# Layer 0's heads 0 and 1 scored one weight chunk before the projection ends

## The reference, cut to what matters

```python
proj = rms_norm(h) @ w_in                      # layer 0: 1024 -> 3072 columns
aq, ak, av, rq, rk, rv, rg = split(proj)       # 8 MoBA heads of 64, 4 retention heads
a_out = softmax(mask(rotary(aq) @ rotary(ak).T / 8)) @ av      # 256 tokens are one block: causal attention
r_out = group_norm((rot(rq) @ rot(rk).T * decay) @ rv) * silu(rg)
h = h + concat(a_out, r_out) @ w_out
h = h + hierarchical_moe(rms_norm(h))          # top 1 of 4 groups, top 2 of its 8 experts
```

## Time and profile before

| | |
|---|---|
| time of the runs, median of 3 | 1108.76 us (1108.43 to 1109.37) |
| the profiled execution, its own time | 1110.2 us |
| its span, first to last instruction | 1108.4 us |
| TensorE's mean granted clock | 0.910 of full speed |
| busy: PE, DVE, ACT, POOL | 903.1, 416.5, 243.8, 41.9 us |
| moved by the DMA engines | 440.73 MB, mean 398 GB/s |

### The profile page before, as it was taken

How to read it: one execution, slowest core, us unless ns; L and a number is a source line. 1 busy time by engine, 2 the same in 40 slices (tenths; PEclk the granted TensorE clock), 3 DMA queues, 4 the chain that set the end, 5 groups by cost and what they waited for, 6 DMA issues and landing times.

```text
span 1108.4 us, 21929 instructions
## 1 busy us (share of the span) xinstructions
PE 903.1 (81%) x9146; PEld 593.1 (54%) x9146; DVE 416.5 (38%) x1006; ACT 243.8 (22%) x622; POOL 41.9 (4%) x65
## 2 busy tenths in 40 slices
PE   9999989978685867677799998999676858585875
PEld 6877745645353535353488676656443525353532
DVE  6888433332222222222288665333221222222222
ACT  5567311100000000000265863111010000000012
POOL 0012200000000000000000312000000000000000
PEclk9999989989887888788999999999887978888899
DMA  9898999999999999999998668999999999999995
GB/s 353 251 402 334 358 410 429 427 429 429 429 428 428 429 427 429 429 429 428 408 386 345 233 270 356 427 427 429 427 430 429 427 428 430 427 428 430 429 426 234
DMA packets 56577, 440.73 MB, mean 398 GB/s; under 512 B 12113, under 2 KB 12625, under 8 KB 31058
## 3 DMA queue, kind: packets, MB, share of 16 engines
q1 hardware_dynamic: 56240, 440.02, 95.7%
q10 hardware_dynamic: 290, 0.07, 0.0%
HBM read 439.03 MB, written 1.05 MB: 397 GB/s over the span
## 4 chain that ended last, share of the span: by engine, by line
PE 49%; DMA 35%; SPq 5%; another core or an unknown queue 3%; DVE 3%; ACT 2%; issue 1%; POOL 0%; POOLq 0%; ACTq 0%; DVEq 0%
DMA ring<-in_w_expert_up 27%; PE banks L1138 14%; DMA ring<-in_w_expert_down 7%; PE banks L1166 6%; PE banks L1106 6%; PE banks L1179 3%; PE banks L1015 3%; PE banks L1019 3%; PE banks L1016 3%; SPq L524 2%; SPq L472 1%; PE banks L1232 1%; PE banks L1234 1%; PE banks L1233 1%
## 5 line engine op out<-in xcount | busy, mean ns | idle before, releaser
L1138 PE MATMUL banks<-ring,scratch 128*32 128x256 f32 x4096 | 287.2, 443 | 129.2 <-DMA ring<-in_w_expert_up 128.8
L1138 PEld LDWEIGHTS banks<-ring,scratch 128*32 128x32 f32 x4096 | 150.3, 127 | 260.2 <-issue 122.2
L1665 DVE TENSOR_SCALAR scratch<-scratch 128x128 f32<-128x128 f32 x64 | 14.5, 227 | 510.3 <-ACT scratch L779 507.6
L1166 PE MATMUL banks<-ring,xn 128*32 128x256 f32 x2048 | 137.0, 410 | 7.7 <-DMA ring<-in_w_expert_down 7.5
L778 ACT ACTIVATE scratch<-banks 128x128 f32<-128x128 f32 x64 | 17.8, 278 | 511.1 <-PE banks L1138 499.7
L1106 PEld LDWEIGHTS banks<-scratch,h 128*128 128x128 f32 x448 | 107.7, 334 | 5.8 <-issue 5.8
L1106 PE MATMUL banks<-scratch,h 128*128 128x128 f32 x448 | 110.4, 405 | 0.0
L1179 PE MATMUL banks<-xn 32*128 32x256 f32 x1024 | 74.8, 403 | 36.5 <-ACT xn L788 36.5
L1166 PEld LDWEIGHTS banks<-ring,xn 128*32 128x32 f32 x2048 | 63.6, 116 | 60.0 <-issue 23.1
L1179 PEld LDWEIGHTS banks<-xn 32*128 32x128 f32 x1024 | 50.3, 186 | 67.8 <-issue 67.7
L1440 DVE SCALAR_TENSOR_TENSOR split<-ring,gains,split 128x512 fp32r<-128x512 f32 x96 | 69.7, 765 | 24.1 <-ACT split L826 23.3
(11 more groups left out here) (177 smaller groups left out, 792.9 us busy)
## 6 DMA issues: line engine op xcount, KB each, us to landing
ring<-in_w_expert_gate SPq DMA_DIRECT2D x62, 2048.0 KB, 45.5
ring<-in_w_expert_up SPq DMA_DIRECT2D x61, 2048.0 KB, 48.8
ring<-in_w_expert_down SPq DMA_DIRECT2D x56, 2048.0 KB, 47.5
ring<-in_w_in_even SPq DMA_DIRECT2D x5, 2048.0 KB, 17.8
ring<-in_w_expert_down SPq DMA_DIRECT2D x10, 1024.0 KB, 10.0
ring<-in_w_in_odd SPq DMA_DIRECT2D x5, 2048.0 KB, 19.7
ring<-in_w_expert_up SPq DMA_DIRECT2D x6, 1024.0 KB, 11.0
ring<-in_w_out_even SPq DMA_DIRECT2D x2, 2048.0 KB, 9.0
```

The costliest lines, as they stand in the source:

```text
L1138: last = pe.matmul(psum[6][32 * j:32 * j + 32, 0:2 * P].rearrange("p (a s) -> p a s", a=2), xT[:, c, SLOTS * k:SLOTS * k + SLOTS], ring[:, ...
L1166: last = pe.matmul(psum[4][32 * q:32 * q + 32, 0:QUARTER], hidT[k][:, 32 * j:32 * j + 32], ring[:, DOWN_AT[k], D * j + QUARTER * q:D * j + ...
```

## The change

Five edits, all in layer 0:

- PE: `scores(0, 0)` stands between chunks 6 and 7 of block 5 instead of behind chunk 7. The wait for the retention scores' banks moves from it to `scores(0, 2)`.
- The two pairs of PSUM banks are swapped for layer 0: heads 0, 1, 4 and 5 in banks 4 and 5, the others in banks 0 and 1. Layer 1's stay as they are.
- DVE: `head_max` 0 and 1 stand ahead of `swish(1, 1)`. Behind it come `head_sum` 0 and 1 and the other maxima and sums in a changed order.
- ACT: exponentials 0 and 1 stand ahead of the `block_out` of block 5, as in layer 1.
- DVE: the gate of the retention's first half (four instructions) stands in one piece behind `head_sum` 7; before, two of the four stood ahead of it.

```diff
--- before.py
+++ after.py
@@ -451,7 +451,7 @@
             return psum[4 + 2 * t + q if ph % 2 == 0 else 2 * (1 - t) + q]
 
         def score_bank(l, m):
-            return psum[m % 2 + (0 if m // 2 % 2 == 0 else 6 if l else 4)]
+            return psum[m % 2 + ((0 if m // 2 % 2 == 0 else 6) if l else (4 if m // 2 % 2 == 0 else 0))]
 
         def mix_bank(n, t):
             return psum[t if n == 0 else 6 + t]
@@ -857,7 +857,7 @@
                             split_hT(l, t, 1)
                     else:
                         parts(0, 4)
-                    if l and j == NW:
+                    if j == NW:
                         for m in range(2):
                             exponentials(l, m)
                     if j > ROTATED[l]:
@@ -885,8 +885,7 @@
                     parts(COPY_AT[1], C)
 
                 if l == 0:
-                    for m in range(3):
-                        exponentials(l, m)
+                    exponentials(l, 2)
                     for m in range(5):
                         exponentials(l, m + 3)
                         copy_pT(l, m)
@@ -1044,7 +1043,7 @@
 
                 if m >= 4:
                     pe.wait_ge(s_out[l], m - 2)
-                elif l == 0 and m == 0:
+                elif l == 0 and m == 2:
                     pe.wait_ge(ret_ready, RET)
                 heads = [(score_bank(l, n), slice(HEAD * (n % 2), HEAD * (n % 2) + HEAD)) for n in (m, m + 1)]
                 q, k = qT[:, m // 2, :], kT[:, m // 2, :]
@@ -1301,9 +1300,12 @@
                     if l == 0 and j == NW - 1:
                         for i in range(2, RET):
                             item_scores(l, i)
-                    project(l, j, TURN_AT[1], C)
+                        project(l, j, TURN_AT[1], C - 1)
+                        scores(l, 0)
+                        project(l, j, C - 1, C)
+                    else:
+                        project(l, j, TURN_AT[1], C)
                 if l == 0:
-                    scores(l, 0)
                     scores(l, 2)
                     for b in range(2, 4):
                         pe.wait_ge(bank_out[l][b], 3)
@@ -1746,30 +1748,29 @@
                     swish(1, 0, link)
                     for n in range(2, RET):
                         decayed(n)
+                    for m in range(2):
+                        head_max(l, m)
                     swish(1, 1, link)
                 else:
                     dve.wait_ge(const_loaded[3], 16)
                 if l == 0:
-                    for m in range(3):
+                    for m in range(2):
+                        head_sum(l, m, link)
+                    for m in range(2, 5):
                         head_max(l, m)
-                    head_sum(l, 0, link)
-                    head_max(l, 3)
-                    head_sum(l, 1, link)
-                    head_max(l, 4)
+                    head_sum(l, 2, link)
                     head_max(l, 5)
-                    head_sum(l, 2, link)
-                    head_max(l, 6)
                     head_sum(l, 3, link)
-                    head_max(l, 7)
+                    for m in range(6, 8):
+                        head_max(l, m)
                     head_sum(l, 4, link)
                     retained_stats(0, link)
                     head_sum(l, 5, link)
                     retained_stats(1, link)
                     head_sum(l, 6, link)
                     retained_variance(link)
-                    retained_gate(0, (0, 1), link)
                     head_sum(l, 7, link)
-                    retained_gate(0, (2, 3), link)
+                    retained_gate(0, range(RET), link)
                     low_oT(0)
                     retained_gate(1, range(RET), link)
                     low_oT(1)
```

## The result

The changed kernel takes 1111.01 us (median of 21 runs, 1109.44 to 1114.01) where the kernel before takes 1109.37 in the same series (21 runs, 1107.81 to 1112.54): a ratio of 1.0014, with a 95% interval of 1.0007 to 1.0020, or +1.6 us. That is slower, and within the 0.2% that was set as the bound of no change. The profiled execution has 1110.56 us around a span of 1108.8, against 1110.2 and 1108.4 before.

The account below looks back on a forecast made before the run. The stream of expert weights, held up by PE's pace in layer 0's mixer, was taken as the bound. +2.03 and -0.47 sum to +1.56 on 1108.76, forecast 1110.3 us, range 1108.7 to 1112.0.

Parts of the forecast that it names:

- Scores, maxima, exponentials: Layer 0, block 5: scores start at 80.21 us, the first maximum at 81.17, the first exponential at 81.85.
- The eviction behind two heads: ACT, block 5: evictions wait for two heads' exponentials, run 83.63 to 85.00, and delay PE's `retain(0)` by 2.03 us.
- The extra break: PE, block 5: scores between chunks 6 and 7 cost about 0.3 us, hidden under PE's wait for the eviction.
- The term of -0.47: Attention's end: `head_sum` 7 directly behind its exponentials runs 0.47 us earlier, shortening PE's wait; bounds 0 to 0.59.
- POOL's late gate product: POOL: the gate's product moves from 81.84 to 84.1 us, covered by `scores` 6; cost nothing, without cover up to 2.3.
- The transfers: SP: two loads behind block 5 come 1.1 us later at no cost; the load at 97.47 goes with the attention.
- The eviction was felt: Against a rival: the eviction does not hold PE, time 1108.6 us; chance 0.13 together with the other no-change case.
- the stream did not hide it: Against a rival: DMA engines catch up PE's loss, time 1108.8 us; chance 0.13 together with the other no-change case.
- The clock did not fall: Against a rival: PE's clock falls behind the new stall, 1.7 us more, time 1112.0 us; chance 0.14.

Follow-up runs that it names:

- experiment 1: Changed kernel with layer 0's last `block_out` back ahead of exponentials 0 and 1 on ACT; ratio to the kernel before 1.0015.
- experiment 2: Changed kernel with only head 0's exponentials ahead of layer 0's last `block_out`, head 1's behind it; ratio to the kernel before 1.0004.
- Experiment 7: Changed kernel with the last `block_out` ahead of exponentials 0 and 1, and maxima 2 and 3 ahead of sums 0 and 1; ratio to before 1.0004.
- experiment 4: Kernel before with only `head_sum` 7 moved ahead of all four gate instructions; ratio to the kernel before 0.9998.
- Experiment 8: Kernel before with `head_sum` 7 ahead of the gate and `low_oT(0)` between the gate's two pairs of instructions; one run, 1108.39 us.
- experiment 3: Changed kernel with `swish(1, 1)` ahead of `head_max` 0 and 1 again; ratio to the kernel before 1.0037.
- experiment 5: Changed kernel with `scores(0)` behind chunk 3 and maxima 0 and 1 ahead of both reciprocals; ratio to the kernel before 0.9996.
- experiment 6: Changed kernel with scores behind chunk 3, maxima ahead of both reciprocals, exponentials 2 to 4 ahead of ACT's copies, `head_sum` 5 ahead of retention statistics; ratio to before 0.9996.

## Why the prediction was right

The forecast was 1108.76 + 1.56, +0.14%; measured were +0.14% in time and +1.53 at the mix and at the stage load. Step by step:

- **Scores, maxima, exponentials.** Forecast at 80.21, 81.17 and 81.85; with this execution's 0.17 taken off 80.04, 81.00 and 81.68. The rows have 80.05, 81.00 and 81.68.
- **The eviction behind two heads.** Forecast to start at 83.63, that is 83.46 with the 0.17 taken off, and found at 83.45. Its length was taken as 1.37 and is 1.24 (83.45 + 1.24 = 84.69): before, the second of the two started at 81.7, just when the block's last matmul had ended (81.28 + 0.39), so the 1.37 held a wait for PE. And PE went on 0.10 behind the eviction instead of 0.14. These two make 0.17 of the 0.18 between +2.03 and the +1.85 found. Experiments 1 and 2 show the cause: no stall with the eviction first, and 0.87 less with one head less.
- **The extra break.** Forecast 0.3, hidden under the stall. Experiment 7 shows it nearly bare at 0.44. Hidden it was: the stall measures 1.38 instead of the 1.7 forecast, and 0.44 + 1.38 is the 1.82 of delay, about the 1.85 of the marks.
- **`head_sum` 7.** The term of -0.47 was mis-sized, by a bound that the prediction had named: PE then waits for the half of pair 0 that DVE makes behind all four gate instructions. The sum did come directly behind its exponentials, and PE's wait of 0.59 fell to 0.11 (about 0.1 forecast), but `values(2)` lost 0.18 to that half, which ends at 95.16 + 0.42 = 95.58, with `values(2)` at 95.73. What is left is 1.53 - 1.85 = -0.32 in the changed kernel and -0.30 in experiment 4. Experiment 8 gives the 0.18 back.
- **POOL's late gate product.** It started at 83.95 (84.1 forecast); from `retain(0)` to the transposes of head 0 the changed kernel needs 3.41 us, before 3.44. It cost nothing.
- **The transfers.** SP's first load behind the block came 1.07 later behind the mark (82.59 - 73.77 against 81.69 - 73.94; forecast 1.1), at no cost, and the load behind the attention 1.66 later (1.8 forecast). Up to there the stream gave nothing back: +1.53 at the stage load, +1.52 in the first load that follows the experts. What became of it behind that is told in the last section.
- **The rivals.** The eviction was felt, and the stream did not hide it in the runs' time. The clock did not fall behind the stall of the changed kernel, in two profiles, and did in experiment 3. The Trainium skill ("TensorE: Matmul & The Clock Gate", "Why this matters for your kernels") warns that idle gaps between bursts of matmuls bring the clock to half; the trace agrees for a PE that stood 1.82 us and not for one that stood 1.38 in the same place. The length of a gap does not decide it alone: in the kernel before, 0.78 us of idle time from 210 us on was followed by 1.2 GHz for a part of the stretch.

Two errors, 0.18 too much on the stall and 0.15 too much on the gain, stood against each other. That the sum is off by only 0.03 at the mix is luck; its terms are not that good.

What stays open: why experiment 1 is timed at 1.0015 when its marks are only 0.53 us behind before.

## What to carry to other kernels

When a consumer is let in early, ask what its engine was about to do at that moment: here ACT's exponentials were not on the path, the eviction that they pushed back was, and each head cost its full length. Moving the producer by one chunk moves it into that crowd; four chunks earlier the same work found ACT idle (for 3.07 us ahead of it in experiment 5). And where a wait at the end of a queue is removed by moving one instruction up, read what is moved down behind it: here that took back 0.18 of the 0.47 us.

## What the runs showed that was not expected

The experts' first stretch runs part of its time at 1.2 GHz, and how much of it differs by execution: the granted clock from 145 to 150 and from 150 to 155 us was 0.50 and 0.59 before, 0.66 and 1.00 in the changed kernel's first profile and 1.00 and 1.00 in its second, 1.00 and 1.00 in experiment 1, 0.63 and 0.69 in experiment 6. The second load of gate weights that follows the experts (L472) comes 82.78 us behind the mark before and 81.29 in the changed kernel, although the first came 1.52 later there. Further on most of the order of the marks is back: at SP's L476 load at 347.97 us of before, the changed kernel is 0.62 and 0.97 behind in its two profiles (1.53 and 1.51 at the stage load), experiment 3 is 2.72 behind (3.52) and experiment 4 is 1.07 ahead (0.29). All four profiles stand 0.5 to 0.9 better against before than at the stage load, so it seems to be the one profile of before that lost time there; that the clock took it fits, but is not shown. The spans of two single profiles (1108.4 and 1108.8) show only 0.4 of the 1.5 us, and the 21 runs of one kernel spread over 4.6 or 4.7 us. So the end is told by the runs alone, and effects of this size by marks that lie ahead of that stretch, which repeat to 0.02 us.

In experiment 3, 0.44 us more of PE idle time came with 1.55 us more behind it, all of it between `retain(0)` and the transposes of head 0 (4.97 us against 3.41), where the clock stood at 1.2 GHz for over 3 us. A stall's price is not only its length.
